# A two-block network in split fp32: the first transfers reordered, and one weight tile's split moved at two boundaries

## The chip, the cores and the metric

One core of a Trainium2 chip runs the whole kernel. The metric is device time in microseconds of one execution. Three runs of the kernel before took 1573.39, 1573.96 and 1577.56 us; the median is 1573.96.

## The reference

The input is x (512 rows of 1024), a condition vector c (1024), and weights. The first block modulates each of its three sublayers by columns computed from c; the second has two mixers without such columns. Cut to what matters here:

```
cs  = silu(c)
mod = cs @ w_ada + b_ada          # w_ada: 1024 x 9216, nine groups of 1024 columns
sh1, sc1, gt1, sh2, sc2, gt2, sh3, sc3, gt3 = mod
h = rms_norm(x, g_ffn1) * (1 + sc1) + sh1
x = x + 0.5 * gt1 * (silu(h @ w_g) * (h @ w_u)) @ w_down      # first FFN, d_ff 2816
h = rms_norm(x, g_mix) * (1 + sc2) + sh2
x = x + gt2 * hybrid_mixer(h)                                 # mLSTM and dilated attention
h = rms_norm(x, g_ffn2) * (1 + sc3) + sh3
x = x + 0.5 * gt3 * swiglu(h)                                 # second FFN
x = rms_norm(x, g_final)
x = x + even_mixer(rms_norm(x))   # pooling and a state space scan
x = x + odd_mixer(rms_norm(x))    # a depthwise convolution of 31 taps
return rms_norm(x, final_norm)
```

## The kernel before

The five engines run programs written out by hand, with semaphores between them. x is kept transposed in SBUF as xT: eight tiles of 128 features by 512 rows. Every large product is computed from values split in a high and a low part: `three` (L2025 to L2027) does three matmuls, hi by hi, lo by hi and hi by lo. So each weight tile (128 x 1024, 512 KB) goes through four steps: SP loads it to w_stage, a ring of four slots, with its semaphore w_loaded; ACT copies it to w_hi (`hi`, L794); DVE subtracts to w_lo (`lo`, L1265) and raises w_split; PE uses it in eight times three matmuls and raises w_used. Tiles are numbered through: 0 and 1 are the first pair of w_gu, T_MIX is the first of the mixer, T_FFN[1] the first of the second FFN.

*The start.* POOL issues the tiles of w_ada (`ada_load`, L545; 512 KB each, eight slots): eight for each group of columns, the group of the scale first, then that of the shift, and then seven more groups. The next tile of a slot is issued when DVE has used the last one. SP issues 14 small rows of constants (L462), five smaller ones (L465, L466), the identity, b_ada, and x (L470), in this order, and then w_gu tiles 0 and 1 after ada_done has reached 8, and tiles 2 and 3 after it has reached 11. PE waits for all constants, transposes them to ps0 and ps1 (L1990, L1991), DVE copies them to cols and bada (L1259, L1261), ACT computes cs from cols (L788). DVE then adds up cs times w_ada tile by tile (`ada_add`, L1275, L1278), eight for each group. PE transposes x in 32 pieces (L1996); ACT copies each eighth to xT (L907) and squares it (L800); PE sums the squares over the partitions with a matmul against ones (L2002), reduces the first ada group and the second (`ada_reduce`, L2019). DVE adds b_ada (`ada_col`, L1284): for the first group this stands after the fifth addition of the second group. After the last addition come `lo` of tiles 0 and 1, the second `ada_col`, `scale_cols`, and `modulate`. On ACT, norm_rs(0) (L831, L833: Ln and Exp) comes first, and then `hi` of tiles 0 and 1.

*The two inner boundaries.* Before the mixer and before the second FFN, PE uses the first tile on x scaled but not yet normalised (`lead`), while the sum of squares, Ln and Exp run; the sum over the partitions is done within it (L2012, L2013). Then ACT runs norm_rs, `hi` of the third tile (T_MIX + 2 or T_FFN[1] + 2), and its part of `modulate` (h_hi, L856). DVE's `modulate` waits for rs, computes the products hn (L1300, tile tmp), and from the third on also h_lo (L1305). After the second product `lo` of the third tile stands between. PE then uses the second and third tile as a pair (`project_pair`), after w_split of both, k by k as h_lo gets ready. At the second FFN, PE has transposes for the mixer's set-up (L2352, L2355) between lead and pair.

## Time and profile before

| | |
|---|---|
| median of three runs | 1573.96 us |
| profiled execution | 1573.8 us, its span 1572.1 us |
| mean granted TensorE clock | 0.985 |
| PE busy | 1479.7 us, 94% |
| DVE busy | 892.2 us, 57% |
| ACT busy | 616.3 us, 39% |
| POOL busy | 383.7 us, 24% |
| DMA | 177.93 MB, mean 113 GB/s |

The span runs from the first to the last instruction of the core. Busy times are of a single profiled execution. PE's busy time counts matmuls at either clock, so its share says nothing of how fast they ran; PEclk in the views does. DMA queue q0 carries what POOL issues, q1 what SP issues. A name in brackets behind a row of the timeline is what ended the engine's idle time before it.

### The profile page before, as it was taken

To read this page: it belongs to the slowest core of one execution; us is meant where nothing else is said; L and a number is where in the kernel's file an instruction comes from. 1 tells how busy PE (TensorE), PEld (TensorE's weight loads), DVE (VectorE), ACT (ScalarE), POOL (GpSimd) and SP (SyncE) were. 2 spreads that over 40 slices of the span, in tenths; PEclk is the share of its full clock that TensorE was granted. 3 is DMA by queue.
4 is the path that set the end of the run, shared out by engine and by line. 5 is a ranking of instruction groups with operands and counts; after the bars stand their busy time and mean duration, and the time that the engine had idled before them with its cause. 6 is when DMAs were issued, how large, how long until landed. Compare 5 with 4: busy or idle time off the path is not lost. (4 is left out here: it accounts for less than half of the span.)

```text
span 1572.1 us, 19033 instructions
## 1 busy us (share of the span) xinstructions
PE 1479.7 (94%) x7031; PEld 1168.1 (74%) x7031; DVE 892.2 (57%) x1269; ACT 616.3 (39%) x928; POOL 383.7 (24%) x494
## 2 busy tenths in 40 slices
PE   4899999999999999899999999999899999989977
PEld 2788888888877776468888888888677787766555
DVE  4777525633573566837534335332656457799964
ACT  3422212222433443744433112222431245777634
POOL 3021101000000000031006788300202100899900
PEclk9899999999999999999999999999999999999979
DMA  9787625333243122013332433553133223222201
GB/s 350 223 278 262 226 82 182 100 105 99 57 126 105 54 68 79 1 36 101 107 100 95 147 94 108 163 206 94 43 92 120 68 87 91 81 68 80 67 27 54
DMA packets 204710, 177.93 MB, mean 113 GB/s; under 512 B 7379, under 2 KB 184079, under 8 KB 204118
## 3 DMA queue, kind: packets, MB, share of 16 engines
q1 hardware_dynamic: 188438, 121.87, 26.2%
q0 software_dynamic: 15040, 52.89, 9.5%
q10 hardware_dynamic: 1152, 2.10, 0.4%
q8 instruction: 51, 0.84, 0.2%
q14 instruction: 29, 0.24, 0.0%
HBM read 168.37 MB, written 8.46 MB: 112 GB/s over the span
## 5 line engine op out<-in xcount | busy, mean ns | idle before, releaser
L2025 PE MATMUL ps<-h_hi,w_hi 128*128 128x512 f32 x1224 | 491.6, 402 | 18.6 <-DVE w_lo L1265 11.1
L2026 PE MATMUL ps<-h_lo,w_hi 128*128 128x512 f32 x1224 | 478.9, 391 | 0.0
L2027 PE MATMUL ps<-h_hi,w_lo 128*128 128x512 f32 x1224 | 478.8, 391 | 0.0
L1265 DVE TENSOR_TENSOR w_lo<-w_stage,w_hi 128x1024 fp32r<-128x1024 f32 x225 | 294.7, 1323 | 222.5 <-ACT w_hi L794 219.9
L794 ACT ACTIVATE w_hi<-w_stage 128x1024 fp32r<-128x1024 f32 x225 | 230.8, 1048 | 190.0 <-PE ps L2027 183.2
L2025 PEld LDWEIGHTS ps<-h_hi,w_hi 128*128 128x128 f32 x1224 | 230.8, 189 | 87.9 <-issue 38.5
L2026 PEld LDWEIGHTS ps<-h_lo,w_hi 128*128 128x128 f32 x1224 | 231.0, 189 | 49.1 <-issue 3.6
L2027 PEld LDWEIGHTS ps<-h_hi,w_lo 128*128 128x128 f32 x1224 | 230.9, 189 | 49.1
L2025 PE MATMUL ps<-a_hi,w_hi 128*128 128x512 f32 x544 | 214.5, 394 | 13.1 <-DVE a_lo L1957 9.4
L2027 PE MATMUL ps<-a_hi,w_lo 128*128 128x512 f32 x544 | 212.9, 391 | 0.0
L2026 PE MATMUL ps<-a_lo,w_hi 128*128 128x512 f32 x544 | 212.8, 391 | 0.0
L1341 DVE TENSOR_TENSOR tmp<-tmp,ps 128x512 f32<-128x512 f32 x44 | 30.3, 688 | 195.4 <-PE ps L2027 195.2
L2025 PEld LDWEIGHTS ps<-a_hi,w_hi 128*128 128x128 f32 x544 | 102.8, 189 | 38.1 <-issue 13.9
L876 ACT ACTIVATE a_hi<-tmp 128x512 fp32r<-128x512 f32 (+1 forms) x44 | 27.8, 633 | 232.9 <-DVE tmp L1341 232.9
L2027 PEld LDWEIGHTS ps<-a_hi,w_lo 128*128 128x128 f32 x544 | 102.8, 189 | 21.7
L2026 PEld LDWEIGHTS ps<-a_lo,w_hi 128*128 128x128 f32 x544 | 102.9, 189 | 21.0
L545 POOL DMA_DIRECT2D ada_w<-in_w_ada x72 | 38.2, 532 | 233.6 <-DVE ada_acc L1275 134.2
L778 POOL TENSOR_TENSOR pacc<-pacc,tmp 128x512 f32<-128x512 f32 x49 | 74.3, 1517 | 63.4 <-ACT tmp L1212 59.4
L1278 DVE SCALAR_TENSOR_TENSOR ada_acc<-ada_w,cs,ada_acc 128x1024 f32<-128x1024 f32 x63 | 80.8, 1283 | 2.6
L1884 DVE SCALAR_TENSOR_TENSOR ps<-gb,cw,ps 128x512 f32<-128x512 f32 x110 | 74.3, 744 | 0.0
L778 POOL TENSOR_TENSOR pacc<-pacc,sq 128x512 f32<-128x512 f32 x48 | 71.9, 1498 | 3.9
L874 ACT ACTIVATE tmp<-ps 128x512 f32<-128x512 f32 x43 | 25.7, 599 | 109.0 <-PE ps L2027 109.0
(433 smaller groups left out, 1497.7 us busy)
## 6 DMA issues: line engine op xcount, KB each, us to landing
w_stage<-in_w_gu SPq DMA_DIRECT2D x88, 512.0 KB, 4.2
ada_w<-in_w_ada POOLq DMA_DIRECT2D x72, 512.0 KB, 6.5
w_stage<-in_w_down SPq DMA_DIRECT2D x44, 512.0 KB, 3.7
w_stage<-in_w_in SPq DMA_DIRECT2D x24, 512.0 KB, 3.9
w_stage<-in_odd_w_in SPq DMA_DIRECT2D x24, 512.0 KB, 3.7
w_stage<-in_even_w_in SPq DMA_DIRECT2D x16, 512.0 KB, 3.8
w_stage<-in_w_out SPq DMA_DIRECT2D x8, 512.0 KB, 3.7
mats<-mats_d POOLq DMA_DIRECT2D x4, 1024.0 KB, 7.2
```

What stands on the lines that cost most here:

```text
L545: pool.dma_start(ada_w[:, kt], a["w_ada"][0][kt * P:(kt + 1) * P, bass.ds(j * D, D)]) \
L778: pool.tensor_tensor(pacc[:, t % 2], pacc[:, t % 2], tap_of[m % 4], ALU.add).then_inc(pool_tap, 1)
L794: act.activation(w_hi[:, c % RING], w_in[:, c % RING], ACT.Copy).then_inc(w_hi_ready, 1)
L874: act.activation(tmp[:, f % 2], ps[2 * (f % 2)][:], ACT.Silu).then_inc(silu_ready, 1)
L876: act.activation(a_hi[:, bass.ds(i * (2 * S) + f * S, S)], tmp2[:, f % 2], ACT.Copy) \
L1265: dve.tensor_tensor(w_lo[:, c % RING], w_in[:, c % RING], w_hi[:, c % RING].bitcast(F32), ALU.subtract).then_inc(w_split, 1)
L1278: dve.scalar_tensor_tensor(acc, ada_w[:, kt], cs[:, kt:kt + 1], acc, ALU.mult, ALU.add).then_inc(ada_done, 1)
L1341: dve.tensor_tensor(tmp2[:, f % 2], tmp[:, f % 2], ps[2 * (f % 2) + 1][:], ALU.mult) \
L1884: dve.scalar_tensor_tensor(acc, gb[:, t % 2, k:k + S], cw[:, t, k:k + 1], acc, ALU.mult, ALU.add).then_inc(tap_done, 1)
L2025: pe.matmul(bank, w_hi[:, slot, k], rhs_hi, start=start, stop=False, skip_group_check=True)
L2026: pe.matmul(bank, w_hi[:, slot, k], rhs_lo, start=False, stop=False, skip_group_check=True)
L2027: return pe.matmul(bank, w_lo[:, slot, k], rhs_hi, start=False, stop=stop, skip_group_check=True)
```

## The change

At the start, SP issues c, the identity and x first (c and the identity on a semaphore of their own, c_in), and then the other constants and b_ada. The waits for ada_done ahead of w_gu tiles 0 and 1 are gone; tiles 2 and 3 wait for 14 additions instead of 11. POOL waits for w_gu 0 and 1 before it issues the third ada group. PE transposes c alone to ps7, and ACT takes silu from there. PE then transposes x (the last eighth after silu), and the other constants behind it, to ps1 and ps2, once ACT has copied three eighths of x. DVE copies them after the first addition of the second group; PE waits for these copies before the first reduction. ACT splits w_gu 0 and 1 ahead of norm_rs(0) instead of behind it.

At the two inner boundaries, ACT's `hi` of the third tile stands ahead of norm_rs, and DVE's `lo` of it ahead of the wait for rs.

```diff
--- before.py
+++ after.py
@@ -375,6 +375,7 @@
         w_hi_ready = sem("w_hi_ready")
         w_split = sem("w_split")
         w_used = sem("w_used")
+        c_in = sem("c_in")
         const_in, x_in, zeroed = sem("const_in"), sem("x_in"), sem("zeroed")
         cols_t, cols_ready = sem("cols_t"), sem("cols_ready")
         x_t, x_ready, silu_c = sem("x_t"), sem("x_ready"), sem("silu_c")
@@ -456,7 +457,10 @@
         @block.sync
         def _(sp):
             sp.wait_ge(zeroed, 1)
-            for name, at, n in ROWS:
+            sp.dma_start(rows[C_C:C_C + KT, :], a["c"].rearrange("a (r q) -> (a r) q", q=P)).then_inc(c_in, 16)
+            sp.dma_start(ident[:], a["ident"]).then_inc(c_in, 16)
+            sp.dma_start(x_rows[:], a["x"][0].rearrange("(t p) d -> p t d", p=P)).then_inc(x_in, 16)
+            for name, at, n in ROWS[1:]:
                 src = a[name]
                 src = src.rearrange("a b -> (a b)") if len(src.shape) == 2 else src
                 sp.dma_start(rows[at:at + n, :], src.rearrange("(r q) -> r q", q=P)).then_inc(const_in, 16)
@@ -465,13 +469,10 @@
                     sp.dma_start(rows[at:at + 1, 64 * k:64 * k + 64], a[name]).then_inc(const_in, 16)
             sp.dma_start(rows[GATE_B:GATE_B + 1, 0:16],
                          a["gate_bias"].rearrange("o g h -> o (g h)")).then_inc(const_in, 16)
-            sp.dma_start(ident[:], a["ident"]).then_inc(const_in, 16)
             sp.dma_start(rows2[0:72], a["b_ada"][0].rearrange("(r q) -> r q", q=P)).then_inc(const_in, 16)
-            sp.dma_start(x_rows[:], a["x"][0].rearrange("(t p) d -> p t d", p=P)).then_inc(x_in, 16)
-
-            def load(i, c, src, late=0):
-
-                upto(sp, ada_done, late)
+
+            def load(i, c, src):
+
                 upto(sp, w_split, i * RING + (c - RING + 1))
                 sp.dma_start(w_in[:, c % RING], src).then_inc(w_loaded[c % RING], 16)
 
@@ -479,9 +480,9 @@
                 for half in range(2):
                     t0, f0 = T_FFN[n] + half * 3 * HALF, half * HALF
                     for j in range(2):
-                        load(0, t0 + j, cols_of(w_gu[n], f0 * P + j * FF), 0 if t0 else KT)
+                        load(0, t0 + j, cols_of(w_gu[n], f0 * P + j * FF))
                     if t0 == 0:
-                        sp.wait_ge(ada_done, KT + 3)
+                        sp.wait_ge(ada_done, 2 * KT - 2)
 
                     def pair_of_hidden(i):
                         for j in range(4):
@@ -548,6 +549,8 @@
             for q in range(2):
                 for kt in range(KT):
                     ada_load(q, ADA_ORDER[q], kt)
+            for c in range(2):
+                pool.wait_ge(w_loaded[c], 16)
             with pool.Fori(2, 9) as j:
                 for kt in range(KT):
                     ada_load(j, j, kt)
@@ -784,8 +787,8 @@
 
         @block.scalar
         def _(act):
-            act.wait_ge(cols_ready, 1)
-            act.activation(cs[:], cols[:, C_C:C_C + KT], ACT.Silu).then_inc(silu_c, 1)
+            act.wait_ge(cols_t, 1)
+            act.activation(cs[:], ps[7][:, 0:KT], ACT.Silu).then_inc(silu_c, 1)
 
             def hi(i, c):
 
@@ -908,9 +911,9 @@
                 if kt:
                     act.wait_ge(x_ready, kt)
                     square(0, kt - 1)
-            norm_rs(0)
             for c in range(2):
                 hi(0, c)
+            norm_rs(0)
             act.wait_ge(mod_ready, 2)
             act.wait_ge(gs_ready, 1)
             modulate(0, sublayer(0)[1])
@@ -1055,8 +1058,8 @@
                     if norm_after == 2:
                         scaled_hi(n, gs[:, 2 * KT:3 * KT])
 
+            hi(0, T_MIX + 2)
             norm_rs(1)
-            hi(0, T_MIX + 2)
             modulate(1, sublayer(1)[1])
             project_posts()
             mlstm()
@@ -1219,8 +1222,8 @@
                 act.activation(pacc[:, t % 2], gb[:, t % 2, 0:S], ACT.Identity, scale=cw[:, t, 0:1],
                                bias=cols[:, CONV_B + t:CONV_B + t + 1]).then_inc(tap_ready, 1)
 
+            hi(0, T_FFN[1] + 2)
             norm_rs(2)
-            hi(0, T_FFN[1] + 2)
             modulate(2, sublayer(2)[1])
             ffn(1, N_FIN, set_up)
             final_and_even_rs()
@@ -1255,10 +1258,6 @@
                 ins.then_inc(dve_self, 1)
                 dve.wait_ge(dve_self, chain[0])
 
-            dve.wait_ge(cols_t, 1)
-            dve.tensor_copy(cols[:], ps[0][:, 0:N_COLS]).then_inc(cols_ready, 1)
-            dve.wait_ge(cols_t, 2)
-            dve.tensor_copy(bada[:], ps[1][:, 0:72]).then_inc(cols_ready, 1)
             def lo(i, c):
 
                 dve.wait_ge(w_hi_ready, i * RING + (c + 1))
@@ -1292,6 +1291,8 @@
 
             def modulate(n, m, scale, shift):
 
+                if m:
+                    lo(0, [None, T_MIX, T_FFN[1]][m] + 2)
                 dve.wait_ge(rs_ready, n + 1)
                 for kt in range(KT + 2):
                     if kt < KT:
@@ -1304,8 +1305,6 @@
                         dve.wait_ge(h_hi_ready, H_NORM[m] * KT + j + 1)
                         dve.scalar_tensor_tensor(h_lo[:, j], hn[j % 4], shift[:, j:j + 1],
                                                  h_hi[:, j].bitcast(F32), ALU.add, ALU.subtract).then_inc(h_ready, 1)
-                    if kt == 1 and m:
-                        lo(0, [None, T_MIX, T_FFN[1]][m] + 2)
 
             def add_square(n, kt):
 
@@ -1397,6 +1396,12 @@
             for q in range(2):
                 for kt in range(KT):
                     ada_add(q, kt)
+                    if q == 1 and kt == 0:
+                        dve.wait_ge(cols_t, 2)
+                        dve.tensor_copy(cols[:], ps[1][:, 0:N_COLS]).then_inc(cols_ready, 1)
+                        dve.wait_ge(cols_t, 3)
+                        dve.tensor_copy(bada[:], ps[2][:, 0:72]).then_inc(cols_ready, 1)
+                        dve.wait_ge(cols_ready, 2)
                     if q == 1 and kt == KT // 2:
                         ada_col(0, ADA_ORDER[0])
             lo(0, 0)
@@ -1985,16 +1990,20 @@
 
         @block.tensor
         def _(pe):
-            pe.wait_ge(const_in, 16 * (len(ROWS) + 4 + 1 + 2))
+            pe.wait_ge(c_in, 32)
             pe.wait_ge(zeroed, 3)
-            pe.transpose(ps[0][:, 0:N_COLS], rows[0:N_COLS, :], ident[0:N_COLS, 0:N_COLS]).then_inc(cols_t, 1)
-            pe.transpose(ps[1][:, 0:72], rows2[0:72, :], ident[0:72, 0:72]).then_inc(cols_t, 1)
+            pe.transpose(ps[7][:, 0:KT], rows[C_C:C_C + KT, :], ident[0:KT, 0:KT]).then_inc(cols_t, 1)
             pe.wait_ge(x_in, 16)
-            pe.wait_ge(cols_ready, 2)
             for kt in range(KT):
+                if kt == KT - 1:
+                    pe.wait_ge(silu_c, 1)
                 for st in range(ST):
                     mm = pe.transpose(ps[kt][:, st * P:(st + 1) * P], x_rows[:, st, kt * P:(kt + 1) * P], ident[:])
                 mm.then_inc(x_t, 1)
+            pe.wait_ge(const_in, 16 * (len(ROWS) - 1 + 4 + 1 + 1))
+            pe.wait_ge(x_ready, 3)
+            pe.transpose(ps[1][:, 0:N_COLS], rows[0:N_COLS, :], ident[0:N_COLS, 0:N_COLS]).then_inc(cols_t, 1)
+            pe.transpose(ps[2][:, 0:72], rows2[0:72, :], ident[0:72, 0:72]).then_inc(cols_t, 1)
 
             def norm_sum(n, kt):
 
@@ -2121,6 +2130,7 @@
                     pe.wait_ge(x_ready, 1)
                 norm_sum(0, kt)
             pe.wait_ge(x_ready, KT)
+            pe.wait_ge(cols_ready, 2)
             ada_reduce(0)
             ada_reduce(1)
             ffn(0, 0, 1, True)
```

## Rows read from the trace of the kernel before

**Rows 1.** The page: busy time, share and instructions of one engine.
```profile
PE 1479.7 (94%) x7031; PEld 1168.1 (74%) x7031; DVE 892.2 (57%) x1269; ACT 616.3 (39%) x928; POOL 383.7 (24%) x494
```

**Rows 2.** Waits of PE, whole span: us in total, times, longest.
```profile
PE ps L2025 <- DVE h_lo L1305: 5.7, 2, 4.2
```

**Rows 3.** Timeline, first 48 us: start, duration, instruction, count, idle time before.
```profile
1.11 0.41 SPq L462 DMA_DIRECT2D rows<-in_c  x1
...
8.53 0.39 SPq L470 DMA_DIRECT2D x_rows<-in_x  x1
...
14.98 0.44 PE L1990 MATMUL ps<-ident,rows 103*128 103x103 f32 x1 [14.98 <-DMA rows<-in_b_ada]
...
16.86 9.62 DVE L1278 SCALAR_TENSOR_TENSOR ada_acc<-ada_w,cs,ada_acc 128x1024 f32<-128x1024 f32 x7
...
20.26 6.34 PE L1996 MATMUL ps<-ident,x_rows 128*128 128x128 f32 x32 [4.73 <-DMA x_rows<-in_x]
...
26.44 7.85 PE L2002 MATMUL ps<-sq,ones 128*128 128x512 f32 x16
...
34.13 1.84 PE L2019 MATMUL ps<-ones,ada_acc 128*128 128x1 f32 x16
...
36.10 4.06 DVE L1278 SCALAR_TENSOR_TENSOR ada_acc<-ada_w,cs,ada_acc 128x1024 f32<-128x1024 f32 x3
...
39.81 1.06 ACT L794 ACTIVATE w_hi<-w_stage 128x1024 fp32r<-128x1024 f32 x1 [4.03 <-DMA w_stage<-in_w_gu]
...
40.21 3.58 PE L2019 MATMUL ps<-ones,ada_acc 128*128 128x1 f32 x16 [4.24 <-DVE ada_acc L1278]
...
44.67 0.16 DVE L1284 TENSOR_TENSOR mod<-ps,bada 128x8 f32<-128x8 f32 x1
...
47.95 0.77 PE L2025 MATMUL ps<-h_hi,w_hi 128*128 128x512 f32 x1 [4.17 <-DVE h_lo L1305]
```

**Rows 4.** DMA queues in microseconds 7, 17, 37 (two) and 49: packets, MB.
```profile
q1 hardware_dynamic: 22, 0.01, 2.7%
...
q1 hardware_dynamic: 100, 0.41, 102.9%
...
q0 software_dynamic: 94, 0.34, 88.4%
...
q1 hardware_dynamic: 93, 0.05, 16.0%
...
q1 hardware_dynamic: 579, 0.29, 120.0%
```

**Rows 5.** Slices of 1 us: length, PE, PEld, DVE, ACT, POOL, PEclk, DMA share, GB/s.
```profile
39.00:40.00 1.00, 0.00 (x0) 0.00 (x0) 1.00 (x1) 0.19 (x1) 0.53 (x1) 0.68 1.02 377
...
436.00:437.00 1.00, 1.00 (x4) 0.73 (x3) 1.00 (x3) 0.40 (x1) 0.00 (x0) 0.50 1.20 293
```

**Rows 6.** Timeline at the boundary to the mixer.
```profile
426.51 1.04 ACT L794 ACTIVATE w_hi<-w_stage 128x1024 fp32r<-128x1024 f32 x1
...
428.33 0.69 ACT L831 ACTIVATE rs<-ps,eps 128x512 f32<-128x512 f32 x1 [0.78 <-PE ps L2013]
...
429.78 1.41 DVE L1300 SCALAR_TENSOR_TENSOR tmp<-xT,gs,rs 128x512 f32<-128x512 f32 x2 [0.91 <-ACT rs L833]
...
431.12 1.22 DVE L1265 TENSOR_TENSOR w_lo<-w_stage,w_hi 128x1024 fp32r<-128x1024 f32 x1
...
432.91 0.74 DVE L1305 SCALAR_TENSOR_TENSOR h_lo<-tmp,mod,h_hi 128x512 fp32r<-128x512 f32 x1
...
433.80 0.47 PE L2025 MATMUL ps<-h_hi,w_hi 128*128 128x512 f32 x1 [1.58 <-DVE h_lo L1305]
```

**Rows 7.** Timeline at the boundary to the second FFN.
```profile
735.64 0.69 ACT L831 ACTIVATE rs<-ps,eps 128x512 f32<-128x512 f32 x1 [1.73 <-PE ps L2013]
...
740.16 0.74 DVE L1305 SCALAR_TENSOR_TENSOR h_lo<-tmp,mod,h_hi 128x512 fp32r<-128x512 f32 x1
...
741.49 0.47 PE L2025 MATMUL ps<-h_hi,w_hi 128*128 128x512 f32 x1
```

## The prediction

> **What bounds the kernel now.** I read the page first: PE is busy 94% of the span [rows 1], so time can only be won where PE stands still or runs at its lower clock. The waits of PE name such places. Of the two that the change aims at, one line is the norm's chain: matmuls of L2025 waited for h_lo of L1305 twice, 5.7 us in all, the longest 4.2 us [rows 2]. The timeline of the first 48 us shows the rest [rows 3]: PE does nothing of weight before 47.95 us, and from there on it has next to no gap in the first FFN. So each microsecond by which the first matmul of L2025 comes earlier is one off the span, as long as weights keep up. The chain that leads to it, backwards: first matmul at 47.95, mod of the second ada column group at 44.67, the 16 small matmuls on ada_acc1 from 40.21 (3.58 us), the last three ada additions from 36.10 to 40.16 on DVE, and these had stood behind the first ada column, which waited for PE's reduction at 34.13, which stands in PE's order behind the eight norm sums (26.44 to 34.13), and those behind the 32 transposes of x (20.26, 6.34 us), which waited for x. x was issued last on SP, at 8.53, and landed by 20.26. The ada additions themselves began only after the constants' transposes at 14.98 and ran without a pause (9.62 us for seven, 1.37 each), so DVE and PE's string came together at 36.
>
> The view of the DMA queues by microsecond says how fast things can come [rows 4]: one queue alone with 4 KB packets moves 100 packets (0.41 MB) per us; alone with the 512 B packets of a w_gu tile 579 (0.29 MB); both at once 94 against 93 packets, turn by turn, so 0.34 MB of ada and 0.05 MB of w_gu. The two inner boundaries are read from timelines around 426 and 735 us [rows 6, 7].
>
> **The change part by part.**
>
> *x and c first.* SP now issues c, ident and x as its first three (x from about 1.95 instead of 8.53). c and ident (8 and 128 small packets) move before the ada tiles are at full rate, and land at about 5. One transpose and silu follow, so ada additions can start when the first tile is there, at about 6.5 instead of 16. x is 512 packets of 4 KB against ada's 4 KB packets. Taking turns as in [rows 4] gives it 50 per us: 10.3 us from about 4.3, so it lands at about 15 instead of 20.3. Bounds: alone it would take 5.1 us and land at 9.5; with a third of the turns, 20. I take 15. PE's transposes then end at 15 + 6.3 = 21.4. Until then the ada additions wait for tiles: 4 by 15 us, and by 0.34 MB/us (1.55 us a tile of 0.524 MB) from there, the sixteenth at about 33.
>
> *The constants after x.* 18 small DMAs and b_ada now queue behind x, and PE waits for them ahead of the norm sums. Lower bound: about 230 packets at 93 per us, 2.5 us, so 17.5. Upper bound: the pace of the same small ones before, 22 packets in a us [rows 4], or about 0.4 us each: 18 x 0.4 + 1 for b_ada = 8.2 us, so 23.5 with the landing. Before, a small DMA was issued only every 0.35 us, which explains most of that pace, while now they stand ready; I take 21.8, just behind x's transposes. The two transposes take 0.5, so the norm sums start at 22.3 instead of 26.44: 4.1 us earlier. From that start to the end of the ada additions everything keeps its order: 26.44 to 34.13 norm sums, reduction, and three additions, to 40.16, are 13.7 us [rows 3]. ACT paces the norm sums in both. So the additions end at 36.0. The copies of cols and bada (0.5 us on DVE, once ahead of all) now stand behind the ninth addition, at about 24, and are hidden, since DVE then waits for the first column until 32.
>
> *What could hold the additions back instead.* The last ada tile at 33 and one addition give 34.5, so 1.5 us of slack to 36.0.
>
> *w_gu 0 and 1.* They were issued after eight additions and w_hi started at 39.81 [rows 3], so the two splits of w_lo stood on DVE ahead of mod until 44.66. Now they are on SP's queue behind the constants, from about 19 to 22, in turns with ada, 93 packets per us until 33, then alone at 579: the second of 1024 packets lands at about 34.5. POOL's further ada loads wait for both, so nothing stretches this. ACT splits them ahead of norm_rs: about 35.6, and then a table load, Ln (0.69 [rows 6]) and Exp, some 2.6 us together in the timeline behind 33.1, to 38.3; they're needed at 39.9, 1.6 us of slack. Their w_lo (2.5 us) lie under the 3.6 us reduction after 36.0. So mod comes 3.7 instead of 4.5 us after the last addition: 0.8 us gained. Then 3.3 us to the first matmul as before: 36.0 + 3.7 + 3.3 = 43.0 instead of 47.95, **4.9 us**.
>
> *The clock there.* After 3.7 us without PE work the granted clock fell to 0.5 (1.2 GHz) in the slice 39 to 40 [rows 5], and the reduction took 3.58 instead of 1.84 us. The gap between the two reductions stays at three additions, so I keep this and the slow first matmuls at no change.
>
> *w_gu 2 and 3, ada's third round.* Issued at about 33 (after 14 additions) and 34.5; 2048 small packets, of which some 900 before ada's tiles join, the others at 93 per us: landed by about 49. PE uses them after the first pair, 48 matmuls or 13 us behind 43.0, at 56, and the split takes 3. Cover of 4 us; without it PE would wait from there. Later tiles follow w_split as before.
>
> *Mix boundary (430 us).* Before [rows 6]: ACT was through w_hi at 427.55, stood idle 0.78 and began Ln at 428.33; DVE began the norm's products at 429.78, did two, then w_lo at 431.12, so the first h_lo at 432.91 and the matmul pair at 433.80, PE having waited 1.58. Now a second w_hi (1.04) stands ahead of Ln: 427.57 to 428.62, Ln 0.29 later, Exp ends 429.97. w_lo on DVE runs from 428.87 to 430.10, so products start at 430.12, 0.34 later, but run without the 1.13 in between: h_lo at 432.12, **0.8 us** earlier. Its SP load was issued long before. Behind the wait for w_hi on DVE stand only those products; PE still had its lead matmuls.
>
> *The clock there.* With that wait the clock fell to 0.5 (the slice from 436 in [rows 5]). Eight matmuls started 0.43 instead of 0.23 us apart: 1.6 us. With half the wait I expect no fall (other single waits of 0.8 to 0.9 us in the trace had none): **1.6 us**. Bounds 0 and 1.6.
>
> *FFN boundary (740 us).* ACT had 1.73 us idle before Ln [rows 7], which takes the w_hi whole. h_lo comes 1.1 us earlier, at 739.0, but PE had its own work (transposes for the set-up) right up to the pair at 741.49, and h_lo (740.16 + 0.74) was there before. **0**, with bounds -0.1 and 0.1.
>
> **Sum.** 4.9 + 0.8 + 1.6 + 0 = 7.3 us. Span 1572.1 - 7.3 = 1564.8; the profiled execution took 1573.8, so 1566.5. The median shown, 1573.96, is the same to 0.2.
>
> **A rule against it.** [Rows 4] show 22 small packets per us under ada's load, without saying on which engines. The Trainium skill (DMA: Bandwidth & Descriptors, Why a DMA increments its semaphore by 16 and not by 1) says that a DMA with fewer rows lies on the lowest-numbered engines alone, so all 18 share the first one. An estimate by it: 18 times two turns behind a 4 KB packet (0.16 us on one engine at 100 packets per us over 16) is 5.8 us, and b_ada after it. No run here shows the engines. It would put the constants at 22 and more, and supports the first rival.
>
> **The rivals.**
>
> *Constants late.* At the old pace they land at 23.5 to 24 and PE stands idle from 21.4. For: the pace of [rows 4]. Against: they were paced by their issue. Norm sums start at 24.4, 2.0 us earlier than before, and after such an idle stretch the clock may be at half: two matmuls of 0.43 us per sum become 1.7 us against ACT's 1.0, about 2 us lost until it rises. Start gain 0.8 to 2.8, boundaries 0.8 to 2.4: 1.6 to 5.2, so 1568.6 to 1572.2.
>
> *The clock falls at the mix boundary all the same.* For: PE is thinly used just before (16 one-column matmuls). Gain 5.7: 1568.1.
>
> *Slower.* The norm sums behind x and constants are the one place: if x gets a third of the turns, it lands at 20, constants at 27, and the norm sums begin at 27.5, at half clock. Eight at 1.7 instead of 1.0 are 5.8 us. First matmul at 47.95 + 1.1 + 5.8 - 0.8 = 54.0, with 0.8 back at the boundary: 1579. It decides once the constants land after 26. Against: equal turns in [rows 4].
>
> *It doesn't do what it says.* If ada's tiles bind (x and w_gu take more of their turns), the additions end at 37.5 and the gain is 5.8: 1568.
>
> **How the numbers follow.** Forecast 0.45, its own range 1564 to 1568; clock falls anyway 0.15; ada binds 0.10; constants late 0.25; slower 0.05. Faster by over 0.3% (4.7 us, about what this measurement can tell) takes the first three and little of the fourth: 0.71. Within 0.3%: 0.24. Slower: 0.05. Range: down to 1564 by the best bounds (x a little earlier, constants right behind), up to 1572.
>
> **What would show it.** First L2025 at 43 +- 1; x transposes at 15; constants' transposes at 21 to 22 with no idle time ahead; additions with gaps for DMA from 6 to 22; first matmul pair at the mix boundary with a wait of 0.8 and no slice at half clock behind it; the pair at the FFN boundary as late behind the lead as before. Wrong if the wait for constants exceeds 2 us, if PE waits for w_lo in the first FFN, or if w_hi 1 comes after 37.

## The result, and the profile after

| | before | after |
|---|---|---|
| median of 5 runs each, us | 1573.96 | 1562.21 |
| lowest to highest, us | 1571.2 to 1578.61 | 1560.36 to 1567.46 |
| ratio, with its 95% interval | | 0.9926 (0.9903 to 0.9948) |
| profiled execution, us (span) | 1573.8 (1572.1) | 1567.46 (1565.8) |

The change makes the kernel 0.74% faster, some 11.6 us. The forecast was 1566.5, with a range from 1564 to 1572. The way was right, the size was not: 7.3 us were forecast, and the median lies 1.8 us under the range. The profiled execution of after was the longest of its five, so the pair of profiles shows only 6.3 us of the gain. This matters below.

The page of after, busy time of the engines, answers to [rows 1]. PE does the same work (two microseconds more is its lower clock, not more matmuls):

```profile
PE 1481.7 (95%) x7032; PEld 1167.9 (75%) x7032; DVE 892.3 (57%) x1269; ACT 616.3 (39%) x928; POOL 384.3 (25%) x494
```

The timeline of the first 42 us of after (start, duration, instruction, count, idle time before and who ended it) answers to [rows 3]. Line numbers moved with the change: L2034 of after is L2025 of before.

```profile
1.99 0.42 SPq L462 DMA_DIRECT2D x_rows<-in_x  x1
...
5.90 0.75 DVE L1274 TENSOR_SCALAR ada_acc<-ada_w,cs 128x1024 f32<-128x1024 f32 x1 [5.90 <-DMA ada_w<-in_w_ada]
...
14.23 6.06 PE L2001 MATMUL ps<-ident,x_rows 128*128 128x128 f32 x32 [10.47 <-DMA x_rows<-in_x]
...
20.78 0.31 PE L2005 MATMUL ps<-ident,rows 103*128 103x103 f32 x1 [0.50 <-DMA rows<-in_b_ada]
...
20.99 7.90 PE L2011 MATMUL ps<-sq,ones 128*128 128x512 f32 x16
...
30.69 4.06 DVE L1277 SCALAR_TENSOR_TENSOR ada_acc<-ada_w,cs,ada_acc 128x1024 f32<-128x1024 f32 x3
31.84 1.06 ACT L797 ACTIVATE w_hi<-w_stage 128x1024 fp32r<-128x1024 f32 x1 [4.12 <-DMA w_stage<-in_w_gu]
34.05 1.06 ACT L797 ACTIVATE w_hi<-w_stage 128x1024 fp32r<-128x1024 f32 x1 [1.15 <-DMA w_stage<-in_w_gu]
34.67 2.35 DVE L1264 TENSOR_TENSOR w_lo<-w_stage,w_hi 128x1024 fp32r<-128x1024 f32 x2
34.80 3.57 PE L2028 MATMUL ps<-ones,ada_acc 128*128 128x1 f32 x16 [4.23 <-DVE ada_acc L1277]
...
37.13 0.63 ACT L836 ACTIVATE rs<-rs 128x512 f32<-128x512 f32 x1
...
38.41 0.17 DVE L1283 TENSOR_TENSOR mod<-ps,bada 128x8 f32<-128x8 f32 x1 [1.39 <-PE ps L2028]
...
41.70 0.76 PE L2034 MATMUL ps<-h_hi,w_hi 128*128 128x512 f32 x1 [3.33 <-DVE h_lo L1306]
```

See how the chain closes up: x at 14.23 and not 20.26, the constants 0.50 us late for PE, the norm sums at 20.99 and not 26.44, both w_lo under the second reduction, and only that reduction ahead of mod. The first matmul of the FFN comes 6.25 us earlier.

The timeline of after at the boundary to the mixer answers to [rows 6]. Ln follows w_hi at once. DVE is in w_lo when rs is there (Exp ends at 423.29), so the products start 0.3 us behind rs, at 423.60, and then run without a split between them:

```profile
420.06 1.99 ACT L797 ACTIVATE w_hi<-w_stage 128x1024 fp32r<-128x1024 f32 x2
...
421.96 0.67 ACT L834 ACTIVATE rs<-ps,eps 128x512 f32<-128x512 f32 x1
...
422.46 1.23 DVE L1264 TENSOR_TENSOR w_lo<-w_stage,w_hi 128x1024 fp32r<-128x1024 f32 x1
...
423.60 2.07 DVE L1301 SCALAR_TENSOR_TENSOR tmp<-xT,gs,rs 128x512 f32<-128x512 f32 x3
...
425.59 0.74 DVE L1306 SCALAR_TENSOR_TENSOR h_lo<-tmp,mod,h_hi 128x512 fp32r<-128x512 f32 x1
...
426.48 0.47 PE L2034 MATMUL ps<-h_hi,w_hi 128*128 128x512 f32 x1 [0.70 <-DVE h_lo L1306]
```

A slice right behind it (length, then busy share and count of PE, PEld, DVE, ACT, POOL, then PEclk) shows the full clock, where [rows 5] had 0.50:

```profile
428.00:429.00 1.00, 1.00 (x6) 0.84 (x5) 1.00 (x3) 0.64 (x1) 0.00 (x0) 1.00 1.12 336
```

At the boundary to the second FFN [rows 7] h_lo begins 2.5 us ahead of PE's use, and PE comes to it behind its own work:

```profile
731.75 0.75 DVE L1306 SCALAR_TENSOR_TENSOR h_lo<-tmp,mod,h_hi 128x512 fp32r<-128x512 f32 x1
...
734.22 0.47 PE L2034 MATMUL ps<-h_hi,w_hi 128*128 128x512 f32 x1
```

The shift of after against before, instruction by instruction: 6.25 at the first matmul of the FFN, 7.32 at the pair behind the mix boundary (426.48 against 433.80), 8.9 at 450 (before had its matmuls at the lower clock there), 7.3 again at 650 (after had a stretch at the lower clock from 626.6 that before did not have), 7.27 at the second FFN's pair, and 6.3 at the end, where after's last stretch at the lower clock was 12.8 us long and before's 9.1.

### The profile page after: what moved, and what is told of

The parts are those of the page before. It is cut to its first block and busy times, and to the rows that moved or that the text cites. A ratio compares the mean times of both kernels' runs of the same rounds, so it can differ in the third digit from the quotient of the medians.

```text
span 1565.8 us, 19036 instructions
## 1 busy us (share of the span) xinstructions
PE 1481.7 (95%) x7032; PEld 1167.9 (75%) x7032; DVE 892.3 (57%) x1269; ACT 616.3 (39%) x928; POOL 384.3 (25%) x494
## 5 line engine op out<-in xcount | busy, mean ns | idle before, releaser
L2034 PE MATMUL ps<-h_hi,w_hi 128*128 128x512 f32 x1224 | 490.7, 401 | 17.0 <-DVE w_lo L1264 11.2
L2034 PEld LDWEIGHTS ps<-h_hi,w_hi 128*128 128x128 f32 x1224 | 230.2, 188 | 86.1 <-issue 37.0
L2034 PE MATMUL ps<-a_hi,w_hi 128*128 128x512 f32 x544 | 214.4, 394 | 13.1 <-DVE a_lo L1962 9.4
L2034 PEld LDWEIGHTS ps<-a_hi,w_hi 128*128 128x128 f32 x544 | 102.8, 189 | 38.2 <-issue 14.0
L2036 PEld LDWEIGHTS ps<-a_hi,w_lo 128*128 128x128 f32 x544 | 102.8, 189 | 21.8
```

The lines of the kernel that those rows point to most:

```text
L2034: pe.matmul(bank, w_hi[:, slot, k], rhs_hi, start=start, stop=False, skip_group_check=True)
L2036: return pe.matmul(bank, w_lo[:, slot, k], rhs_hi, start=False, stop=stop, skip_group_check=True)
```

## The experiments

Kernels of one batch ran on the same chip with runs of the kernel before among them (their medians: 1575.21, 1575.49, 1572.99 and 1573.65 in batches 1 to 4). The last columns are read from each kernel's one profile: when the first matmul of the FFN started, what PE waited at the mix boundary, whether a stretch at half clock began behind that, and how many us from 60 on were at half clock (the last stretch counted whole, though it runs some 2 us past the end of the span). A ratio within 0.2% of another shows little by itself: base_again is the kernel before without an edit, and its median lies 3.7 us above that of the runs beside it.

| kernel | batch | median us (runs) | ratio to before, 95% | first FFN matmul | mix: wait, half clock | half clock from 60, us | span |
|---|---|---|---|---|---|---|---|
| before (first profile) | - | 1573.96 (5) | | 47.95 | 1.6, yes | 36.3 | 1572.1 |
| base_again | 1 | 1578.88 (12) | 1.0017 (0.9996 to 1.0038) | 52.24 | 1.6, yes | 48.0 | 1578.4 |
| base_p3, base_p4 | 4 | 1571.20, 1572.42 (1 each) | | 48.26, 52.10 | 1.6, yes; 1.6, no | 34.3, 30.7 | 1569.5, 1570.7 |
| after (first profile) | - | 1562.21 (5) | 0.9926 | 41.70 | 0.7, no | 43.4 | 1565.8 |
| after_again | 1 | 1562.54 (6) | 0.9926 (0.9900 to 0.9953) | 41.83 | 0.7, no | 30.8 | 1558.6 |
| after_third | 3 | 1562.92 (6) | 0.9920 (0.9899 to 0.9942) | 42.28 | 0.7, no | 32.9 | 1562.5 |
| start_only | 1 | 1564.48 (11) | 0.9945 (0.9924 to 0.9966) | 41.40 | 1.6, yes | 50.2 | 1569.8 |
| bound_only | 1 | 1571.95 (12) | 0.9979 (0.9960 to 0.9999) | 48.03 | 0.7, no | 37.7 | 1570.4 |
| base_hold | 2 | 1569.74 (12) | 0.9972 (0.9949 to 0.9994) | 46.61 | 1.6, no | 30.8 | 1565.5 |
| hold_bound | 4 | 1568.79 (12) | 0.9968 (0.9952 to 0.9983) | 47.76 | 0.7, no | 34.1 | 1567.1 |
| no_hold | 2 | 1570.70 (10) | 0.9979 (0.9958 to 0.9999) | 49.47 | 0.7, no | 31.1 | 1568.6 |
| w_late | 2 | 1563.11 (6) | 0.9927 (0.9901 to 0.9954) | 41.73 | 0.7, no | 41.2 | 1563.6 |
| x_late | 2 | 1571.93 (10) | 0.9981 (0.9961 to 1.0001) | 51.44 | 0.7, no | 34.1 | 1570.5 |
| adds_late | 3 | 1570.52 (10) | 0.9979 (0.9961 to 0.9998) | 48.86 | 0.7, no | 30.9 | 1566.1 |
| warm | 3 | 1561.60 (6) | 0.9916 (0.9894 to 0.9938) | 41.60 | 0.7, no | 32.9 | 1559.9 |
| warm_norm | 3 | 1561.23 (6) | 0.9912 (0.9891 to 0.9933) | 41.33 | 0.7, no | 32.9 | 1559.5 |
| warm_three | 4 | 1558.65 (6) | 0.9903 (0.9880 to 0.9925) | 40.37 | 0.7, no | 34.2 | 1558.9 |

**The kernel before, again** (base_again, base_p3, base_p4: no edit) **and the kernel after, again.**

> The kernel before, unchanged, profiled once more with the span and mean granted clock of each of its runs. Theory (the clock's slices decide what is beyond 7.3 us): its runs spread over several us, and span and mean clock move together: a mean clock lower by 0.002 (3.1 us more of the span at half clock) goes with some 1.5 us more; whether the slice at half clock behind the mix boundary (near 435 us) is there differs between profiles or is there again. Rival (something outside the clock, such as transfers, is slower in the profiled execution): spans differ by over 2 us at the same mean clock. Median 1571 to 1576.

> The changed kernel, unchanged, profiled once more. Its first profile has half-clock slices of 6.8 us near 627 us, which the kernel before had not, and 12.8 instead of 9.1 us at the end. Theory: in a second profile these are not where they were, the span is 1558 to 1562, and until 430 us it is as in the first (first matmul of the FFN at 41.7 within 0.4, wait of 0.7 at the mix boundary). Its span at the mean clock of the kernel before (0.984 to 0.985) lies 7 to 9 us under it. Rival: the first FFN or a later stage is shorter by over 1 us with no difference in the clock.

> A third profile of the kernel before. Theory (w_gu 1 comes by chance of the sharing): w_hi 1 starts at 42.4 or at 46 to 47, and the first matmul of the FFN 5.5 us behind it, whichever it is. Rival: the late tile of the second profile was an exception, and it is at 42.4 now with a span of 1575 or more all the same.

> A fourth profile of the kernel before, with the same question: w_hi 1 at 42.4 or at 46 to 47, the first matmul 5.5 us behind. With four profiles the mean lateness of w_gu 1 over 42.4 is 1 to 3 us if both occur.

base_again's median of 1578.88 missed its expected 1571 to 1576, and a mean clock lower by 0.002 went with some 2.8 us and not with 1.5 (the two groups below: 0.005 and 7.0 us). after_again, base_p3 and base_p4 came about as expected. The repetition told more than any edit. In the first profile of before the second w_gu tile came just in time; in this one it came late. Its timeline, where w_hi of the first profile stood at 42.44 and mod at 44.67:

```profile
46.73 1.06 ACT L794 ACTIVATE w_hi<-w_stage 128x1024 fp32r<-128x1024 f32 x1 [5.80 <-DMA w_stage<-in_w_gu]
47.82 1.23 DVE L1265 TENSOR_TENSOR w_lo<-w_stage,w_hi 128x1024 fp32r<-128x1024 f32 x1 [5.63 <-ACT w_hi L794]
48.96 0.16 DVE L1284 TENSOR_TENSOR mod<-ps,bada 128x8 f32<-128x8 f32 x1
```

The reason stands in the DMA queues (packets, MB, share). In microsecond 41 of the first profile of before, ada's queue ran dry and w_gu had the engines to itself:

```profile
q1 hardware_dynamic: 558, 0.28, 113.3%
q0 software_dynamic: 6, 0.02, 6.6%
```

In base_again ada still took turns with it at 44:

```profile
q0 software_dynamic: 99, 0.34, 87.7%
q1 hardware_dynamic: 97, 0.05, 16.8%
```

Of four profiles of before two are like the one (first FFN matmul at 47.95 and 48.26) and two like the other (52.24 and 52.10). What tips it is small. POOL asks for five tiles of ada's third round while the shift group is added up, pauses, and asks for the last three behind the first of the last three additions. w_gu 1 has the engines to itself only in the gap that this pause leaves. In the first profile of before the pause ended here:

```profile
38.02 0.53 POOL L545 DMA_DIRECT2D ada_w<-in_w_ada  x1 [4.15 <-DVE ada_acc L1278]
```

In base_again PE was through with x and the norm sums 0.9 us earlier, and so were the additions, and the pause was shorter:

```profile
37.16 0.53 POOL L545 DMA_DIRECT2D ada_w<-in_w_ada  x1 [2.83 <-DVE ada_acc L1278]
```

It ended at 38.02, 37.89 and, in bound_only, 38.32 where the tile was on time, and at 37.16 and 36.88 where it was late: an earlier PE made the first matmul 4.2 us later.

**Two groups of executions.** The spans and mean granted clocks of all runs show something that the medians hide. In batch 1 the 28 runs of before fall into two halves: 14 with a mean clock of 0.984 or more and a median span of 1570.3, and 14 with 0.982 or less and 1577.2. base_again has 9 of 12 in the lower clock's group, start_only 4 of 11 (1562.7 against 1568.3), and bound_only and after_again none of 18. Over all batches 57 of 128 runs with the boundaries as before had 0.982 or less, and 10 of 77 with the new ones (warm, warm_norm and warm_three left out), seven of them in no_hold and adds_late (in both profiles the first stretch at half clock is 20.5 us long, where after has 13.7; that alone lowers the mean by 0.002). So how often the lower group comes goes with the boundaries' order in the main, and not only with it. Why it comes stays open. A median of a kernel with two groups depends on how many runs fall in each, so below the groups are compared as well.

**The start alone, the boundaries alone.** start_only is after with both boundaries as before; bound_only is before with only this:

```diff
+            hi(0, T_MIX + 2)
             norm_rs(1)
-            hi(0, T_MIX + 2)
...
+                if m:
+                    lo(0, [None, T_MIX, T_FFN[1]][m] + 2)
                 dve.wait_ge(rs_ready, n + 1)
...
-                    if kt == 1 and m:
-                        lo(0, [None, T_MIX, T_FFN[1]][m] + 2)
```

> The changed start with both inner boundaries as before. Theory: first matmul at 41.7, so 6.2 us less than before, and nothing else: 1567 to 1568.5, apart from the slices at half clock. At the mix boundary PE waits 1.6 us. Rival (the boundaries bring nothing beyond their 0.9): this one lies within 1 us of the changed kernel.

> The two boundaries as changed, the start as before. Theory: PE waits 0.7 instead of 1.6 us at the mix boundary (0.9 gained), no slice at half clock behind it (up to 1.6 more), nothing at the FFN boundary: 1571.4 to 1573. Rival (the clock falls there all the same, by chance of time): only 0.9, 1573.

The start is 8.7 us (0.55%, interval 5.3 to 12.0), the boundaries 3.3 (0.2 to 6.4); together 12.0, and the whole change measured 11.7 on the same chip. They add. My start had been 4.9, my boundaries 2.4. So what I missed is in the start. At like clock it is 7.6 us in the higher group (span 1570.3 to 1562.7) and 8.9 in the lower (1577.2 to 1568.3). The boundaries alone bring 0.6 at like clock; the rest of their 3.3 is that bound_only has no run in the lower group. bound_only came as expected, start_only 2.5 us under the 1567 to 1568.5 that I had expected of it.

**POOL's hold alone.** base_hold is before with the two lines that keep ada's third round behind w_gu 0 and 1; no_hold is after without them:

```diff
                 for kt in range(KT):
                     ada_load(q, ADA_ORDER[q], kt)
+            for c in range(2):
+                pool.wait_ge(w_loaded[c], 16)
             with pool.Fori(2, 9) as j:
```

> The kernel before with one piece of the change: POOL waits for w_gu 0 and 1 before the third round of ada loads. In the second profile of the kernel before, w_gu 1 came at 46.7 instead of 42.4 us, because its 512 B packets shared the engines with ada's 4 KB packets turn by turn. Theory (the sharing costs 0 to 4.3 us from execution to execution): with the hold w_hi 1 starts by 42.5 at the latest, the first matmul of the FFN is at 46.5 to 48 and the runs lie at 1567 to 1573, with none at 1576 and above. Rival (the slow runs of the kernel before come from slices at half clock later on): the cluster at 1576 to 1582 stays, also with w_gu 1 on time.

> The changed kernel without POOL's wait for w_gu 0 and 1. Theory: ada's third round then joins from about 24 us, one tile at each addition, and the 2048 small packets of w_gu 0 and 1 get only every other turn, 93 per us from about 18.5: w_hi 1 starts at about 41 instead of 34, and the first matmul comes at 45 to 47 instead of 41.7, 3.5 to 5 us more in the total: 1566 to 1568. Rival (early issue is enough): first matmul at 41.7 and 1562.5.

This is the part that I had priced at nothing. Two lines in the kernel before bring 0.28% (4.4 us, interval 0.9 to 8.0), and the change without them keeps 0.21% of its 0.74%. In part base_hold came as its rival said: 5 of its 12 runs still lie at 1575.1 to 1576.1, with a clock of 0.981 or 0.982, so a late tile is not needed for the lower group. Compared at like clock the two lines are worth 1.9 us in the higher group (1569.3 to 1567.4) and 3.1 in the lower (1577.1 to 1574.0). In the timeline of no_hold the second w_gu tile takes until 42.75, though it was asked for at 9:

```profile
31.66 1.06 ACT L795 ACTIVATE w_hi<-w_stage 128x1024 fp32r<-128x1024 f32 x1 [3.80 <-DMA w_stage<-in_w_gu]
...
42.75 1.06 ACT L795 ACTIVATE w_hi<-w_stage 128x1024 fp32r<-128x1024 f32 x1 [10.03 <-DMA w_stage<-in_w_gu]
...
44.98 0.16 DVE L1281 TENSOR_TENSOR mod<-ps,bada 128x8 f32<-128x8 f32 x1
```

I had expected 41 for this split, 45 to 47 for the first matmul and 1566 to 1568 in all; it was 42.75, 49.47 and 1570.70. In this kernel Ln and Exp stand behind the late split on ACT, and the norm's products waited 1.2 us for them besides.

In base_hold both tiles were there in time, and their w_lo lie under the reduction:

```profile
35.19 1.99 ACT L796 ACTIVATE w_hi<-w_stage 128x1024 fp32r<-128x1024 f32 x2
...
39.57 2.35 DVE L1267 TENSOR_TENSOR w_lo<-w_stage,w_hi 128x1024 fp32r<-128x1024 f32 x2
39.71 3.58 PE L2021 MATMUL ps<-ones,ada_acc 128*128 128x1 f32 x16 [4.23 <-DVE ada_acc L1280]
43.33 0.17 DVE L1286 TENSOR_TENSOR mod<-ps,bada 128x8 f32<-128x8 f32 x1 [1.40 <-PE ps L2021]
```

**Hold and boundaries, the old order of transfers** (hold_bound: bound_only with the two lines above).

> The kernel before with the hold on POOL and with both boundaries as changed, but with the first transfers in their old order. Theory (parts add up): first matmul at 46.6, 0.9 and usually 1.6 us back at the mix boundary: 1566 to 1568.5, so 4.5 to 5 us behind the changed kernel, which is what the order of the first transfers is worth once the tiles are not late. Rival (the hold has most of the gain): within 2 us of the changed kernel.

0.32%, or 5.0 us (2.7 to 7.6). Its first matmul came at 47.76 and not at 46.6: x was there 0.6 us later than in base_hold. Against after's 0.9926 some 6.5 us are left for the order of the transfers (first matmul 47.76 against 41.70), where I had expected 4.5 to 5. That the boundaries add their part to base_hold does not show here: 0.9 us between medians of different batches, and base_hold had no half clock behind its wait of 1.6.

**w_gu 0 and 1 issued late** (w_late: after, with SP's wait for 8 additions put back, the hold kept).

```diff
+                        if t0 == 0 and j == 0:
+                            sp.wait_ge(ada_done, KT)
                         load(0, t0 + j, cols_of(w_gu[n], f0 * P + j * FF))
```

> The changed kernel with the hold, but w_gu 0 and 1 issued only after eight additions, as before. Theory: the order on DVE and the hold do it and not the early issue; the tiles start at about 24.5 instead of 18, share until ada's sixteenth tile is there near 32.5 and move alone after it: w_hi 1 at 35 to 36, its w_lo done by 38.2, under the reduction. First matmul within 0.4 of 41.7, 1562.5. Rival (early issue counts): first matmul over 1 us later.

0.9927 and a first matmul at 41.73: no difference. The early issue is worth nothing here; what counts is who shares the engines with the tile while it is under way.

**x behind the constants** (x_late) **and the additions late** (adds_late: DVE waits for the constants' transposes before the first addition).

```diff
-            sp.dma_start(x_rows[:], a["x"][0].rearrange("(t p) d -> p t d", p=P)).then_inc(x_in, 16)
...
             sp.dma_start(rows2[0:72], a["b_ada"][0].rearrange("(r q) -> r q", q=P)).then_inc(const_in, 16)
+            sp.dma_start(x_rows[:], a["x"][0].rearrange("(t p) d -> p t d", p=P)).then_inc(x_in, 16)
```

```diff
             dve.wait_ge(silu_c, 1)
+            dve.wait_ge(cols_t, 3)
```

> The changed kernel with x issued behind the constants instead of ahead of them. Theory (PE's string of transposes of x, constants and norm sums sets the end of the additions): x is issued at about 8.9, shares with ada until its tiles and lands at about 19 to 20; transposes to 25.5, norm sums from 25.7 instead of 21.0, additions end at 39.5, first matmul at 46.3, total 4.6 us more: 1567. Rival (DVE or the ada tiles set it): less than 2 us more.

> The changed kernel with the additions of ada held back until the constants are transposed, as before, so c first is without use. Theory: the additions begin at 21.1 instead of 5.9, but all tiles of the first round lie ready, 1.37 us each: the first eight end at 32, the last at 43.5, the second reduction and mod behind it: first matmul at 50.5, 8.8 later, 1571. The ada queue is idle from 16 to 22, so x lands as before or 1 us earlier. Rival (PE's string sets the end, additions have slack): less than 3 us more.

Each half of the new order alone brings nothing beyond the hold and the boundaries (0.9981 and 0.9979, where hold_bound has 0.9968). x_late was 5 us worse than I had expected: its x was issued at 9.04 and PE began on it only at 24.45, 15.4 us later, where before needed 11.7 [rows 3]. The timeline of x_late:

```profile
24.45 6.29 PE L2001 MATMUL ps<-ident,x_rows 128*128 128x128 f32 x32 [20.79 <-DMA x_rows<-in_x]
```

With c first the additions free ada's slots from 6 us on, so ada keeps its queue full and takes turns with x (53 packets against 48 in microsecond 16, 55 against 56 in 22), while before it had filled its eight slots and paused, and x had microsecond 18 to itself with 102. In adds_late x is there at 14.30, but the thirteen additions up to ada_col run without a gap from 20.79 and end at 37.7, behind everything that mod needs besides:

```profile
21.66 9.62 DVE L1277 SCALAR_TENSOR_TENSOR ada_acc<-ada_w,cs,ada_acc 128x1024 f32<-128x1024 f32 x7
...
37.84 4.06 DVE L1277 SCALAR_TENSOR_TENSOR ada_acc<-ada_w,cs,ada_acc 128x1024 f32<-128x1024 f32 x3
```

**The clock at the start.** With the rest of the start closed up, the second reduction still runs at half clock (1.2 instead of 2.4 GHz), and so do the FFN's first matmuls. warm puts four matmuls of ones by xT, whose results nobody reads, behind each reduction; warm_norm has norm_rs(0) ahead of the two splits besides; warm_three has only three behind the second reduction.

```diff
             ada_reduce(0)
+            for _ in range(4):
+                pe.matmul(ps[5][:], ones[:], xT[:, 0], start=True, stop=True)
             ada_reduce(1)
+            for _ in range(3):
+                pe.matmul(ps[5][:], ones[:], xT[:, 0], start=True, stop=True)
```

> The changed kernel with matmuls of no use on PE in its two idle stretches ahead of the first FFN (four of ones by xT, eight hardware matmuls or 3.4 us, into the unused bank 5, before the second reduction, and four behind it). Theory (3.6 us of the start are the half clock): the granted clock stays at 1.0 from 30 to 60 us, the second reduction takes 1.84 instead of 3.57 us; the norm's Exp (ending at 37.8) then sets the first product, so the first matmul is at 40.8, 0.9 earlier, and its first eleven matmuls start 0.23 to 0.24 instead of 0.43 us apart, 2.2 us: 3.1 us in all, 1559.4. Rival (h_lo, one per 1.33 us, sets the pace of these matmuls at either clock): only 1 us or less of the 2.2, so 1 to 2 us in all. Rival, slower: the extra matmuls hold up the reduction or the pair, 1 us more than the changed kernel.

> The same, with norm_rs(0) ahead of the splits of w_gu 0 and 1 on ACT, as in the kernel before. Theory: the Exp ends at about 30.5, so w_lo (ending at 37.0) and the reduction set mod at 37.0, and the first matmul is at 40.3, 0.5 earlier than with warm alone: 1558.9. Rival (the table load and Ln hold up the split of w_gu 0): no difference from warm, or later.

> The changed kernel once more, beside the two that keep PE warm. Both theories: median 1560 to 1563.5, first matmul of the FFN at 41.7, w_gu 1 split by ACT at 34 to 34.5.

> As warm_norm, with three instead of four extra matmuls behind the second reduction. In warm_norm they ran at half clock for their greater part (5.4 us) and held the pair back to 41.3, while its first h_lo was there at 40.0. Theory: three end at 36.5 + 4.0 = 40.5 or earlier, the first matmul is at 40.2 to 40.6, the clock is at 1.0 again 3 us later at most: 0.8 us less than warm_norm, 1560.4. Rival (less work leaves the clock low for longer): the first matmuls run at half clock, and it is 1 us more than warm_norm.

In warm and warm_norm the reduction takes 1.95 instead of 3.57, but the clock falls just behind it, the four added matmuls (eight entries) last 5.38, and the FFN's first matmul stands in PE's order behind them. In warm_three the three end before h_lo is there, and no stretch at half clock came at all. Its timeline:

```profile
34.96 1.95 PE L2028 MATMUL ps<-ones,ada_acc 128*128 128x1 f32 x16 [0.70 <-DVE ada_acc L1277]
...
36.76 2.82 PE L2139 MATMUL ps<-xT,ones 128*128 128x512 f32 x6
...
40.37 0.47 PE L2034 MATMUL ps<-h_hi,w_hi 128*128 128x512 f32 x1 [0.79 <-DVE h_lo L1306]
```

That the clock held here is not the work of three instead of four. The slices of microsecond 37 (PEclk is the last but two) show warm_norm already at half clock, and warm_three at full:

```profile
37.00:38.00 1.00, 1.00 (x3) 0.35 (x2) 0.93 (x3) 0.00 (x0) 0.74 (x3) 0.50 0.89 316
```

```profile
37.00:38.00 1.00, 1.00 (x3) 0.42 (x3) 0.93 (x4) 0.00 (x0) 0.82 (x2) 1.00 1.00 335
```

The clock fell at 36.9 in warm_norm, 0.4 us into the first added matmuls, and up to there PE's program is the same in both. What three instead of four surely does is to let the first real matmul start at once: h_lo was there at 40.0 in warm_norm and its matmul came at 41.33, at 40.2 and 40.37 in warm_three. None of the three came where I expected it: warm and warm_norm were 2.2 and 2.3 us slower, warm_three 1.8 us faster.

warm_three is the fastest of all: 1558.65 in the median (1557.16 to 1562.02) where after had 1562.2 to 1562.9 in its three sets of runs. The two ratios' intervals overlap, so the last 3 to 4 us rest on the medians and on the profile (span 3.6 us under after_third's).

## Why the prediction was right in its way and wrong in its size

*x first.* Right. Forecast 15, read 14.23. The additions wait for tiles, 4 of them by 15 us, and the last three run without a wait, so ada did not bind.

*The constants.* Right in kind; in size my time was 1.0 too late: I took 21.8 and they were there at 20.78, 6.6 us behind x, where I had 6.8. So most of the 1.0 is x, which came 0.8 earlier. The two transposes delayed the norm sums by 0.2 instead of 0.5. So these began at 20.99 and not at 22.3, and this is the 1.3 us by which the first matmul beats my 43.0. PE's wait for the constants was 0.50. The rival *constants late* is out, and with it *slower*. The prediction's second estimate for the constants, 22 and more, went by what the Trainium skill (DMA: Bandwidth & Descriptors, Why a DMA increments its semaphore by 16 and not by 1) says, that a DMA with few rows lies on the lowest-numbered engines. Counted from where x landed, its 5.8 us end at 20.0 with b_ada still to come, so 20.78 doesn't speak against the rule, and no view shows the engines.

*From norm sums to mod.* Right: 13.7 us to the end of the additions (20.99 to 34.75), then 3.66 to mod against my 3.7. w_gu 1 was split from 34.05 (forecast 34.5), rs was there 1.0 us ahead of its use at 38.81 (forecast slack 1.6).

*Mix boundary.* Right: the wait fell from 1.58 to 0.70, and in all twelve profiles with the new order no stretch at half clock began behind it. With the old one it did in four of six: so my 1.6 us is worth some 1.1 on average. The longer wait goes with these stretches in the profiles; by what rule the clock falls they don't show.

*FFN boundary.* Right: the shift is 7.3 us on both sides of it.

**The step that failed** is "POOL's further ada loads wait for both, so nothing stretches this", with the gain of 0.8 for w_gu 0 and 1. The hold did what I said; what I got wrong is what it replaces. I treated it as cover for the new, early transfer, and priced the old way from the one profile of before, where w_gu 1 happened to land in the pause of ada's third round. So my term of 0.8 us for w_gu 0 and 1 stands for 0.8 us in executions like that one and for 5.0 in the others, 2.9 on average. The other mis-sized term is the norm sums' start, 5.4 us earlier where I had 4.1. [Rows 4] had the warning: with both queues at work w_gu gets 0.05 MB per us, alone 0.29. A tile of 512 KB that is not through when ada starts again waits for several ada tiles. base_again and base_p4 show it (first matmul 4.2 us later than in the other two), base_hold and no_hold show that the hold is what prevents it, and w_late that the early issue isn't.

The sum again, from the profiles: start 6.25, plus 4.2 in two of four executions, 2.1; boundary 0.9; clock there 1.1. That is 10.3 us, where 7.3 were forecast and 11.6 (8.2 to 15.3) measured.

**Of the rest,** part is the clock elsewhere. base_again and base_p4 have the same start to 0.14 us, and base_again is 7.7 us longer with 17.3 us more at half clock: 0.45 us for each. That price is of one pair of profiles. By it the spans of the table, cleared of their half-clock stretches from 60 us on, are 1554.1 to 1556.9 for the four profiles of before, and 1544.7 to 1547.7 for the three of after. The means, 1555.9 and 1546.2, stand 9.6 us apart, which is near 6.25 + 2.1 + 0.9. The runs of batch 1 at a clock of 0.984 or more say the same: median span 1570.3 for before, 1560.9 for after_again, 9.4 apart. What is left of the 11.6 is that before has more such stretches than after: half of its runs lie in the lower group there, and 1 of 17 of after. At the mix boundary they go with PE's longer wait, and bound_only shows that the boundaries' order alone takes the lower group away in its batch. For the other stretches, which come and go between executions of one kernel (at 184, 641, 681, 1114, 1402), the reason stays open, and two us of the difference with them.

## What to carry to other kernels

A transfer that is just in time in one profile may be late in the next: look at what its queue neighbours do in the next few microseconds, and at a second profile, before pricing what happens to it. When two queues take turns packet by packet, try holding the one with large packets back while a tile in small packets is under way; the two lines for it were worth 4.4 us alone (1.9 to 3.1 at like clock), and 8.3 within the change. This reorder of transfers paid only when both consumers that meet at the end (PE's string behind x, and DVE's behind c) were moved together. And look at the clock of every run before comparing medians: an edit can change how often a kernel falls in its longer group, and two kernels with such groups differ by how their runs fall.

## What the runs showed of the hardware

- Taking turns is by packets, whatever their size: 94 packets of 4 KB against 93 of 512 B in a microsecond of before, 97 against 96 in after, 99 against 97 in base_again, 94 against 93 in no_hold. The queue with the small packets gets 0.05 MB per us instead of 0.28.
- 18 rows and b_ada, queued behind x, were there 6.6 us after x, in part under ada's load. In before, with x behind them, the last of them took 6.9 us from its issue (8.11 to 14.98).
- Half-clock stretches come and go between executions of the same kernel, and alone make 7.7 us of 1570 (base_again against base_p4). The runs of the kernel before in batch 1 form two groups by them, 1570.3 and 1577.2 us in the median span. A PE wait of 1.6 us with little work ahead of it was followed by one in four of six profiles, a wait of 0.7 in none of twelve.
- Sixteen one-column matmuls take 3.57 us at half clock and 1.84 to 1.95 at full. With matmuls without use ahead of it the reduction took 1.95 us in all three kernels that had them; behind it the clock fell for 3.4 us in two of the three.
